# Dilated attention in a one-core block: where the bias loads stand, how probabilities are scaled, and how the output product is formed

## The reference, cut to what matters

```python
def dilated_window_attention(h, w_in, w_out, rel_table):
    qkv = (h @ w_in).reshape(B, S, 3, DSWA_HEADS, E)
    ...
    for gi, (window, dil) in enumerate(DSWA_CONFIGS):      # (128,1) (512,4) (2048,16)
        bias = jnp.take(rel_table, rel_bucket(rel), axis=0)[..., hs]
        o, lse = banded_attention(...)                     # softmax(q k / 8 + bias) v, masked
    alpha = jax.nn.softmax(jnp.stack(lses, axis=2), axis=2)
    o = (o * alpha[..., None].astype(o.dtype)).reshape(B, S, DSWA_WIDTH)
    return o @ w_out                                       # 256 x 1152 by 1152 x 1024
```

## Time and profile before

| | us |
|---|---|
| median of three runs | 2258.18 |
| the profiled execution, its own time | 2260.04 |
| its span, first to last instruction | 2258.2 |
| PE busy in the span | 2058.4 (91%) |
| DVE busy | 1333.3 (59%) |
| ACT busy | 882.9 (39%) |
| POOL busy | 73.2 (3%) |
| mean DMA rate | 139 GB/s |

### The profile page before, as it was taken

One profiled execution on the slowest core, in us unless ns is written; L12 is line 12 of the kernel. 1 busy time (PEld: TensorE's weight loads), 2 busy tenths in 40 slices (PEclk: granted clock), 3 DMA queues, 4 the chain that ended last, 5 costly groups with the idle time before them and its releaser, 6 DMA issues. The chain is left out here.

```text
span 2258.2 us, 32684 instructions
## 1 busy us (share of the span) xinstructions
PE 2058.4 (91%) x13620; PEld 1883.6 (83%) x13620; DVE 1333.3 (59%) x2035; ACT 882.9 (39%) x1107; POOL 73.2 (3%) x64
## 2 busy tenths in 40 slices
PE   7968898998999999999997998899689989688997
PEld 7967797898999998888886895899589879558986
DVE  5545664798888886555554964553456343324643
ACT  5445432344444334444444435222055334223532
POOL 0000000000000000000000000552000000000000
PEclk9979899999999999999998989999899989788999
DMA  6523244354444445555553432000144434503543
GB/s 221 177 102 112 94 165 158 145 187 149 146 147 148 147 148 199 187 199 190 190 200 128 147 110 82 1 1 1 57 149 167 186 151 171 129 29 147 178 160 140
DMA packets 48635, 313.11 MB, mean 139 GB/s; under 512 B 5214, under 2 KB 10334, under 8 KB 11904
## 3 DMA queue, kind: packets, MB, share of 16 engines
q1 hardware_dynamic: 47808, 310.66, 38.6%
q10 hardware_dynamic: 576, 0.55, 0.1%
q0 software_dynamic: 128, 0.14, 0.0%
HBM read 309.20 MB, written 2.13 MB: 138 GB/s over the span
## 5 line engine op out<-in xcount | busy, mean ns | idle before, releaser
L310 DVE TENSOR_TENSOR s_ring_lo<-s_ring,s_w_hi 128x2048 fp32r<-128x2048 f32 x231 | 529.0, 2291 | 292.6 <-ACT s_w_hi L304 292.1
L304 ACT ACTIVATE s_w_hi<-s_ring 128x2048 fp32r<-128x2048 f32 x231 | 440.0, 1905 | 119.6 <-PE bank L347 69.3
L347 PE MATMUL bank<-s_hT_hi,s_w_hi 128*128 128x256 f32 x2320 | 341.0, 291 | 14.4 <-PEq L361 9.5
L347 PE MATMUL bank<-s_hT_hi,s_ring_lo 128*128 128x256 f32 x2320 | 332.1, 287 | 9.8 <-DVE s_ring_lo L310 9.7
L347 PEld LDWEIGHTS bank<-s_hT_hi,s_w_hi 128*128 128x128 f32 x2320 | 306.8, 197 | 23.0 <-issue 22.1
L347 PEld LDWEIGHTS bank<-s_hT_hi,s_ring_lo 128*128 128x128 f32 x2320 | 305.2, 196 | 11.2 <-DVE s_ring_lo L310 11.2
L1315 PE MATMUL bank<-s_w_hi,s_hT_lo 128*128 128x512 f32 x1024 | 242.7, 389 | 0.3 <-issue 0.3
L1315 PEld LDWEIGHTS bank<-s_w_hi,s_hT_lo 128*128 128x128 f32 x1024 | 192.3, 188 | 40.2 <-issue 0.4
L347 PE MATMUL bank<-s_hT_lo,s_w_hi 128*128 128x256 f32 x1296 | 189.5, 291 | 0.0
L347 PEld LDWEIGHTS bank<-s_hT_lo,s_w_hi 128*128 128x128 f32 x1296 | 174.9, 201 | 0.0
L347 PE MATMUL bank<-s_x_r,s_w_hi 128*128 128x256 f32 x1024 | 143.8, 283 | 0.0
(11 more groups left out here) (337 smaller groups left out, 2593.1 us busy)
## 6 DMA issues: line engine op xcount, KB each, us to landing
s_ring<-weights SPq DMA_DIRECT2D x282, 1024.0 KB, 4.8
s_arena<-bias_by_distance SPq DMA_DIRECT2D x12, 384.0 KB, 7.1
s_arena<-consts SPq DMA_DIRECT2D x1, 1792.0 KB, 9.3
s_arena<-mem SPq DMA_DIRECT2D x1, 1024.0 KB, 6.2
s_x<-x SPq DMA_DIRECT2D x1, 1024.0 KB, 13.8
x_away<-s_x SPq DMA_DIRECT2D x1, 1024.0 KB, 4.8
s_arena<-sub_keys SPq DMA_DIRECT2D x1, 1024.0 KB, 7.1
s_arena<-x_away SPq DMA_DIRECT2D x1, 1024.0 KB, 8.0
```

The lines of the kernel that those rows point to most:

```text
L304: act.activation(k.w_hi[:, u % 2, :], k.ring[:, u % RING, :], ACT.Copy).then_inc(k.hi_ready, 1)
L310: dve.tensor_tensor(k.ring_lo[:, u % RING, :], k.ring[:, u % RING, :], plain(k.w_hi[:, u % 2, :]), ALU.subtract).then_inc(k.lo_ready, 1)
L347: last = pe.matmul(out[:, nb * S:(nb + 1) * S], w[:, c, nb * P:(nb + 1) * P], h[:, c, :], start=(n == 0 and c == 0), stop=(n == 2 and c == 7))
```

## The change: what it does

There are three edits, in one diff.

1. The biases of the first two turns are loaded in `ds_project`, by POOL behind its own write of the table (`load_bias`), into the same two buffers, which now lie below the projection's working tiles. SP loads those of the turns 2 to 5 as before.
2. The 128x768 scaling of the probabilities is dropped. DVE builds `diag`, the identity times the reciprocal sums (two instructions of 128x128), and PE turns a block by a product with `diag` as the moving operand, not by a transpose with the identity.
3. The output product is made from halves. ACT's two copies of a turn now write the rounded half of the attention's output, DVE subtracts to get the other (`split_o`), and the five weight units are split. The units of the output weights 0 and 1 are split inside the turns 0 and 1, the others behind the last turn. PE goes unit by unit, three products each, into eight half banks, and DVE adds eight pieces of 128x256 to x.

ACT's rounding of unit 0 follows the exponential of turn 0, that of unit 1 the output copies of turn 0. The diff, cut to its core:

```diff
@@ ds_project
-    d.oT = lay.take(9, S)
+    d.oT = [k.mid_r.rearrange("p a c s -> p (a c) s")[:, lay.at // S + 9 * n:lay.at // S + 9 * n + 9, :] for n in range(2)]
+    lay.take(18, S)
+    d.bias = lay.take(2, len(DS_DIL), TT * S)
...
+            pool.wait_ge(k.bias_stored, 16)
+            for j in range(2):
+                load_bias(k, pool, j, bias_here)
...
+def load_bias(k, queue, j, here):
+    G = len(DS_DIL)
+    for tt in range(TT):
+        src = bass.AP(k.bias_dram.tensor, j * DELTAS + tt * P, [[1, P], [DS_PER * DELTAS, G], [1, S]])
+        queue.dma_start(k.ds.bias[:, j % 2, :, tt * S:(tt + 1) * S], src).then_inc(here, 16)
@@ ds_attend, sync
-            sp.wait_ge(k.bias_stored, 16)
-            for j in range(J):
...
+            for j in range(2, J):
+                sp.wait_ge(scaled, G * (j - 1))
+                load_bias(k, sp, j, here[j % 2])
@@ ds_attend, tensor
-                            last = pe.transpose(ps[3 + g][:, kt * S + tt * P:kt * S + (tt + 1) * P],
-                                                sc[:, j % 2, g, tt, kt * P:(kt + 1) * P], k.ident)
+                            last = pe.matmul(ps[3 + g][:, kt * S + tt * P:kt * S + (tt + 1) * P],
+                                             sc[:, j % 2, g, tt, kt * P:(kt + 1) * P], diag[:, j % 2, tt, :],
+                                             start=True, stop=True)
...
+            pe.wait_ge(o_round, 2 * J)
+            for n in range(5):
+                hi, lo = unit_parts(k, F + n)
+                blocks = range(8 * n, min(8 * n + 8, 36))
+                for m, (o, w) in enumerate(((d.oT[0], hi), (d.oT[1], hi), (d.oT[0], lo))):
+                    split_ready(k, pe, F + n, m)
+                    if m == 1 and n == 0:
+                        pe.wait_ge(o_split, 2 * J)
+                    for i in blocks:
+                        c = i % 9
+                        for tt in range(TT):
+                            last = pe.matmul(ps[2 * (i // 9) + tt][:, 0:S], o[:, c, tt * P:(tt + 1) * P],
+                                             w[:, i % 8, :], start=(m == 0 and c == 0), stop=(m == 2 and c == 8))
@@ ds_attend, scalar
+                if j < 2:
+                    split_hi(k, act, F + j)
+            for n in range(2, 5):
+                split_hi(k, act, F + n)
@@ ds_attend, vector
-                    last = dve.tensor_scalar(sc[:, j % 2, :, tt, :], sc[:, j % 2, :, tt, :],
-                                             stat[:, o + 6 + tt:o + 7 + tt], None, ALU.mult)
+                    last = dve.tensor_scalar(diag[:, j % 2, tt, :], k.ident, stat[:, o + 6 + tt:o + 7 + tt], None,
+                                             ALU.mult)
...
+                if j >= 1:
+                    split_o(j - 1)
+                if j < 2:
+                    split_lo(k, dve, F + j)
+            split_o(J - 1)
+            for n in range(2, 5):
+                split_lo(k, dve, F + n)
+                if n >= 3:
+                    add(n - 3)
+            add(2)
+            add(3)
```

More of the change, by code:

```diff
@@ L2302, in ds_project @@
     ds_out, bias_here, bias_mm, bias_ready = (ctx_sem(k, n) for n in names)
+    d.bias_here = bias_here
     with k.nc.Block() as block:
@@ L2361, in ds_attend @@
     lay = Layout(k, d.at)
-    bias = lay.take(2, G, TT * S)
+    bias = d.bias
+    here = [ctx_sem(k, f"ds_bias_here{n}") for n in range(2)]
     sc = lay.take(2, G, TT, S)
@@ L2365, in ds_attend @@
     stat = k.small[:, 16:48]
[L2366 to L2369, removed]
+    diag = lay.take(2, TT, P)
+    names = ("ds_scores", "ds_scaled", "ds_maxed", "ds_exped", "ds_probs",
+             "ds_turned", "ds_pt_out", "ds_pv", "ds_o_round", "ds_o_split")
+    (scores, scaled, maxed, exped, probs, turned, pt_out, pv, o_round, o_split) = (ctx_sem(k, n) for n in names)
     own = Count(ctx_sem(k, "ds_dve"))
@@ L2414, in weigh @@
                 if j >= 1:
-                    pe.wait_ge(pv_out, 2 * j)
+                    pe.wait_ge(o_split, 2 * j)
                 for g in range(G):
@@ L2430, in _ @@
                     weigh(j - 1)
[L2431 to L2441, removed]
+            pe.wait_ge(o_round, 2 * J)
[11 more added lines that the diff above has]
+                                             w[:, i % 8, :], start=(m == 0 and c == 0), stop=(m == 2 and c == 8))
                 last.then_inc(k.unit_done, 1)
-            done_mark(k, pe, k.unit_done)
         @block.scalar
@@ L2464, in _, with split_o, add @@
                     c = (j - 1) // 2
-                    act.activation(d.oT[rows, c:c + 4:3, :], halves(ps[6][rows, :]), ACT.Copy).then_inc(pv_out, 1)
-                    act.activation(d.oT[rows, c + 6, :], ps[7][rows, 0:S], ACT.Copy).then_inc(pv_out, 1)
+                    act.activation(d.oT[0][rows, c:c + 4:3, :], halves(ps[6][rows, :]), ACT.Copy).then_inc(o_round, 1)
+                    act.activation(d.oT[0][rows, c + 6, :], ps[7][rows, 0:S], ACT.Copy).then_inc(o_round, 1)
+                if j < 2:
+                    split_hi(k, act, F + j)
+            for n in range(2, 5):
+                split_hi(k, act, F + n)
         @block.vector
         def _(dve):
+            def split_o(j):
+                rows = slice(E * (j % 2), E * (j % 2) + E)
+                c = j // 2
+                for n, (at, src) in enumerate(((slice(c, c + 4, 3), halves(ps[6][rows, :])),
+                                               (slice(c + 6, c + 7), ps[7][rows, 0:S].rearrange("p (a s) -> p a s", a=1)))):
+                    dve.wait_ge(o_round, 2 * j + n + 1)
+                    dve.tensor_tensor(d.oT[1][rows, at, :], src, plain(d.oT[0][rows, at, :]), ALU.subtract)\
+                       .then_inc(o_split, 1)
+            def add(p):
+                dve.wait_ge(k.unit_done, F + (2, 3, 4, 5)[p])
+                for tt in range(TT):
+                    xs = k.x[:, tt, p * S:(p + 1) * S]
+                    own.up(dve.tensor_tensor(xs, xs, ps[2 * p + tt][:, 0:S], ALU.add))
             for j in range(J):
                 o = 16 * (j % 2)
-                dve.wait_ge(here[j % 2], 16 * TT * (j // 2 + 1))
+                if j < 2:
+                    dve.wait_ge(d.bias_here, 48 + 16 * TT * (j + 1))
+                else:
+                    dve.wait_ge(here[j % 2], 16 * TT * (j // 2))
                 if j >= 2:
@@ L2595, in program @@
     ds_attend(k)
-    k.whole_units += FIRST["mlp1_1"] - FIRST["ds_out"]
     normalise(k, k.x, col(k, "g_mlp1", KC), None, 0, split=(k.hT_hi, k.hT_lo, FIRST["mlp1_1"]))
```

## The result

The changed kernel took 2246.01 us (median of six runs, 2242.29 to 2246.82) against 2258.22 us of the kernel before. The ratio is 0.9942, with a 95% interval of [0.9929, 0.9955]; a second set of runs later gave 0.9947 [0.9934, 0.9961].

| | before, us | after, us | difference |
|---|---|---|---|
| ahead of the stage (unchanged code) | 1930.0 | 1930.7 | +0.7 |
| the stage | 117.5 | 108.1 | -9.3 |
| behind the stage (unchanged instructions) | 210.7 | 206.3 | -4.4 |

A forecast was written before the change was run, and what follows sets the result against it. The attention stage was taken as bound by a chain through PE, DVE and ACT, no single engine. Terms -5.9 + 2.7 + 3.6 + 0.6 + 1.3 - 5.0 + 0.5 - 5.3 + 0.2 = -7.3 us gave 2250.9 us, range 2246 to 2257.5.

The forecast's parts named there:

- behind the stage: Stage after the output product: starts at half clock; where the clock rises can shift, 0, within 1.5 us either way.
- bias of turns 0 and 1: Start of the attention stage: early loads by POOL remove DVE's wait for the bias, -5.9 us.
- split in turn 0: Turn 0: next bias sum waits for ACT's rounding and DVE's subtraction, 4.3 us in place of 1.56, +2.7 us.
- split in turn 1: Turn 1: copies, rounding, subtraction and bias sums take 7.1 us behind weigh(0) in place of 3.5, +3.6 us.
- subtractions of `split_o`: Turns 2 to 4: DVE's subtractions delay the bias sums by 0.2 us each, +0.6 us in all (0 to 1.2).
- weigh(2) to weigh(4), clock: Turns 2 to 4: longer turning product shortens PE's idle time, 1.7 us gained each, -5 us (0 to -7.7).
- weigh(1) and weigh(0), clock: Turns 0 and 1: weigh(0) left at 4.49 us; weigh(1) slower after nearly 6 us idle, +0.5 us.
- output product: After the attention turns: 216 float32r products take 25.9 us where 144 records took 31.35, -5.3 us.
- rival 1: Attention weighs: 2.7 us of idle time still lets PE's clock fall, clock term 0; 2255.9 us, chance 0.22.
- rival 2: Attention weighs: clock kept throughout, every weigh from the third on takes 2.77 us; 2248.2 us, chance 0.15.
- rival 3: Attention turns: PE becomes the bound at clock 0.50, three turns 3 us longer each; 2264.9 us, chance 0.04.
- rival 4: Projection: early bias loads collide with weight units or land late, 5.9 us back; 2256.8 us, chance 0.04.

The follow-up runs named there:

- edit 2 alone: Kernel before with only the scaled identity `diag` and turning by real products added: stage 110.0 us against 117.5, ratio 0.9963 to the kernel before.
- the splits ahead: Changed kernel with ACT's rounding of weight units 0 and 1 before the exponential, DVE's subtraction during it: stage 96.7 us against 108.1, ratio 0.9917 to the kernel before.

## Why the prediction was wrong

The direction was right, and so was the mechanism inside the stage; the time fell just out of the range, by a part that I had put at nothing. By its own terms, in the order of its sum (predicted, measured in the profiles, us):

| term | predicted | measured |
|---|---|---|
| bias of turns 0 and 1 | -5.9 | -6.0 |
| split in turn 0 | +2.7 | +2.5 |
| split in turn 1 | +3.6 | +3.3 |
| subtractions of `split_o` | +0.6 | -0.2 |
| last turning product | +1.3 | +1.3 |
| weigh(2) to weigh(4), clock | -5.0 | -6.0 |
| weigh(1) and weigh(0), clock | +0.5 | +0.9 |
| output product | -5.3 | -5.2 |
| last addition | +0.2 | +0.1 |
| behind the stage | 0, within 1.5 | -4.4 |
| ahead of the stage | none | +0.7 |

**The step that failed is "Behind the stage: where in it the clock rises can shift: 0, within 1.5 either way".** It measured -4.4 us. I had looked at one row, the first products behind the stage at 0.50, priced it at 2.5 us, and then bounded its shift by 1.5 with no reason given; the changed kernel did not pay these 2.5 us at all. Another 1.6 us lie at a place that I had not looked at, the first products of the last matrix after an idle time of 2.48 us (9.18 or 7.55 us). Over all profiles here the rest took 205.9 to 210.7 us with the same instructions. The term had to be bounded by 5 us, and the kernel before lay at its slow end, where a shift could only gain. That 210.7 was the slow end could not be seen from one profile; that it held half-clock stretches at two places could. With the -4.4 at 0 the sum would have been inside the range. Why the change moved it from the slow end to the fast one, and not to the middle, is not shown.

The rest of the miss, 2 us, is in the stage: 1.0 of it is the weighs' clock, mis-sized within its bounds, 0.8 the subtractions, 0.5 the splits' hand-overs, less 0.4 for weigh(1). The subtractions do stand in series with the bias sums, and these ended 3.5 to 3.6 us behind the weigh, near the 3.7 I had worked out; but before, they ended 3.6 us behind it in these turns too, where I had taken the 3.5 us of a turn whose score ran at full clock for all. That the weighs' term came within 1.0 us is partly luck: I had taken 1.7 us for each of three, and they gave 2.6, 0.9 and 2.6. The rivals fell as the rows above say: the clock was kept in part (not rival 1, not rival 2), PE never was the bound (before weigh it was idle for at least 2.45 us, rival 3), and the projection's PE did not wait (rival 4). The measured time is nearer to rival 2's 2248.2 us than to the forecast, but not by its mechanism.

Not shown: why 2.45 us of idle time before a weigh went with 4.46 us in one turn and with 2.77 us in another of the same kernel (edit 2 alone). These runs did not control when the clock fell. It was not chance from one execution to the next either: in all five profiles of the changed kernel and of its variants with the product, weigh(3) took 4.46 us, and weigh(2) and weigh(4) 2.77.

## What to carry to other kernels

In a chain that goes through several engines, an instruction that is put "beside" a wait must stand ahead of the wait in its engine's order: the same two splits cost 6.6 us more behind the exponential than in front of it. PE's idle time counts twice here, once as time and once as the clock of the work behind it; filling it with work that is thrown away took 6.1 us off three weighs. And a stage that ends at another moment can change the clock of what follows: bound that by all the stretches behind it that begin after idle time, not by the nearest. Last, time more executions than the one that is profiled: a profile can be the shortest of its kernel's executions, as it was with the splits ahead.

## What the hardware showed that I had not expected

Twenty-four float32 transposes kept TensorE's clock up as well as twelve full float32 products did (9.6 against 10.0 us for the three weighs behind them). The same instructions took between 205.9 and 210.7 us behind the stage, and nearly the same time again in a second profile of one kernel (206.3 and 206.2). Four loads of 384 KB, issued by POOL in 3.1 us into a stretch with a DMA share of 0.49, left PE's work there as it was.
